# High and low parts of the up and down projections' weights, made for two units in one operation

## The reference, cut to what matters

```
h = rms_norm(x, norm2_w) * (1.0 + sc2) + sh2                     # 256 x 2048
u = causal_depthwise_conv(h @ w_up, conv_w, conv_b)              # w_up: 2048 x 11264
gate, up = u[..., :D_FF], u[..., D_FF:]                          # D_FF = 5632
x = x + g2 * ((silu(gate) * up) @ w_down)                        # w_down: 5632 x 2048
return rms_norm(x, final_norm_w)
```

## Time and profile before

| | us |
|---|---|
| three runs | 1325.77, 1335.37, 1335.42 (median 1335.37) |
| the profiled execution, its own time | 1326.2 |
| its span, first to last instruction | 1324.4 |
| up projection, PE from first to last matmul | 580.35 to 1069.9 |
| down projection, PE from first to last matmul | 1073.77 to 1312.07 |

### The profile page before, as it was taken

The page is one execution under the profiler, slowest core; times in us unless marked ns, Lnnn a source line. Parts: engine busy times, 40 slices in busy tenths (PEclk is TensorE's granted clock), DMA queues, the critical chain, the costliest instruction groups (busy, mean ns, idle before and its releaser), DMA issues.

```text
span 1324.4 us, 20876 instructions
## 1 busy us (share of the span) xinstructions
PE 1274.0 (96%) x7330; PEld 1123.7 (85%) x7330; DVE 997.0 (75%) x1277; ACT 612.8 (46%) x809; POOL 51.3 (4%) x99
## 2 busy tenths in 40 slices
PE   4899999999999999979999999999999999999996
PEld 4898999998998778868888888888888878888885
DVE  3787698998877788878887888788777765545453
ACT  3333654444546654455444444444444443434342
POOL 2000000022121000000000000000000000000000
PEclk9689999999999999989999999999999999999998
DMA  9999688888778789849777777777666675555552
GB/s 339 387 385 359 227 308 270 259 278 271 251 255 275 258 299 387 295 122 320 246 243 231 241 233 238 235 236 225 191 189 190 190 264 196 193 191 193 195 195 100
DMA packets 151716, 329.77 MB, mean 249 GB/s; under 512 B 11237, under 2 KB 11990, under 8 KB 150754
## 3 DMA queue, kind: packets, MB, share of 16 engines
q1 hardware_dynamic: 147856, 318.09, 72.3%
q0 software_dynamic: 3360, 9.98, 2.1%
q10 hardware_dynamic: 434, 0.83, 0.2%
HBM read 323.09 MB, written 4.19 MB: 247 GB/s over the span
## 4 chain that ended last, share of the span: by engine, by line
PE 85%; DVE 5%; ACT 3%; DMA 3%; issue 3%; SPq 0%; DVEq 0%; ACTq 0%
PE bank L1179 24%; PE bank L1181 13%; PE bank L1200 6%; PE bank L1201 6%; PE bank L1202 6%; PE bank L946 5%; PE bank L948 5%; PE bank L947 5%; PE bank L935 3%; PE bank L933 3%; PE bank L936 3%; DMA pc<-in_w_ada 2%; DVE acc_c L1303 2%; PE bank L980 1%; PE bank L967 1%
## 5 line engine op out<-in xcount | busy, mean ns | idle before, releaser
L618 ACT ACTIVATE whi<-wraw 128x1024 fp32r<-128x1024 f32 x408 | 432.2, 1060 | 631.9 <-PE bank L1181 234.7
L1291 DVE TENSOR_TENSOR wlo<-wraw,whi 128x1024 fp32r<-128x1024 f32 x404 | 493.8, 1223 | 258.0 <-ACT whi L618 255.9
L1179 PE MATMUL bank<-h,whi 128*128 128x512 f32 x1408 | 489.5, 392 | 2.7 <-issue 2.7
L1181 PE MATMUL bank<-h,wlo 128*128 128x256 f32 x1408 | 394.8, 280 | 0.0
L1179 PEld LDWEIGHTS bank<-h,whi 128*128 128x128 f32 x1408 | 264.0, 187 | 60.9 <-issue 2.9
L1181 PEld LDWEIGHTS bank<-h,wlo 128*128 128x128 f32 x1408 | 266.8, 189 | 0.0
L933 PE MATMUL bank<-h,whi 128*128 128x256 f32 x512 | 149.3, 292 | 3.3 <-DVE h L1316 3.3
L935 PE MATMUL bank<-h,whi 128*128 128x256 f32 x512 | 146.5, 286 | 0.0
L936 PE MATMUL bank<-h,wlo 128*128 128x256 f32 x512 | 146.5, 286 | 0.0
L1200 PE MATMUL bank<-whi,act_hi 128*128 128x512 f32 x352 | 137.0, 389 | 0.3 <-DVE evt L1580 0.3
L1202 PE MATMUL bank<-whi,act_lo 128*128 128x512 f32 x352 | 136.9, 389 | 0.0
(11 more groups left out here) (223 smaller groups left out, 1305.7 us busy)
## 6 DMA issues: line engine op xcount, KB each, us to landing
wraw<-in_w_up SPq DMA_DIRECT2D x176, 512.0 KB, 4.4
araw<-in_w_ada SPq DMA_DIRECT2D x128, 512.0 KB, 5.2
wraw<-in_w_in SPq DMA_DIRECT2D x112, 512.0 KB, 4.4
wraw<-in_w_down SPq DMA_DIRECT2D x88, 512.0 KB, 3.8
pc<-in_w_ada SPq DMA_DIRECT2D x64, 512.0 KB, 11.4
wraw<-in_w_out SPq DMA_DIRECT2D x32, 512.0 KB, 6.0
x<-in_x SPq DMA_DIRECT2D x2, 1024.0 KB, 6.8
x<-in_x POOLq DMA_DIRECT2D x1, 2048.0 KB, 11.9
```

The source lines that it names most:

```text
L618: act.activation(whi[:, slot], wraw[:, slot], ACT.Copy).then_inc(s_hi, 1)
L1179: pe.matmul(out, whi[:, slot, k, cols], h[:, kk].rearrange("p a t -> p (a t)"), start=(kk == 0), stop=False, skip_group_check=True)
L1181: last = pe.matmul(out[:, 0:SEQ], wlo[:, slot, k, cols], h[:, kk, 0, :], start=False, stop=(kk == KT - 1), skip_group_check=True)
L1291: dve.tensor_tensor(wlo[:, slot], wraw[:, slot], whi[:, slot].bitcast(F32), ALU.subtract).then_inc(s_lo, 1)
```

## The change

On ACT, `hi_pair` replaces `hi_part` from the ninth unit of the up projection to the end of the down projection: at even j one operation of 2048 elements for the slots `slot` and `slot + 1`, which waits for both loads and for PE to be through with the older unit of the second slot (`slot_free(..., j + 1)`), and adds 2 to `s_hi`. On DVE, `lo_pair` does the same for the low parts and adds 2 to `s_lo`. At odd j neither engine splits anything. SP, PE, POOL and all other work keep their code. The units of the input and output projections and the first eight of the up projection are still made singly.

```diff
--- before.py
+++ after.py
@@ -617,9 +617,17 @@
                     act.wait_ge(s_pe, ready)
                 act.activation(whi[:, slot], wraw[:, slot], ACT.Copy).then_inc(s_hi, 1)
 
+            def hi_pair(slot, count, ready):
+
+                act.wait_ge(s_w[slot], count)
+                act.wait_ge(s_w[slot + 1], count)
+                act.wait_ge(s_pe, ready)
+                act.activation(whi[:, slot:slot + 2], wraw[:, slot:slot + 2], ACT.Copy).then_inc(s_hi, 2)
+
             def hi_ahead(ph, unit0, i, j, pe0, loads):
 
-                hi_part((unit0 + j) % RING, i * loads + ((unit0 + j) // RING + 1) * 16, slot_free(ph, pe0, j))
+                if j % 2 == 0:
+                    hi_pair((unit0 + j) % RING, i * loads + ((unit0 + j) // RING + 1) * 16, slot_free(ph, pe0, j + 1))
 
 
             act.wait_ge(s_prmT, 1)
@@ -851,8 +859,8 @@
                         act.wait_ge(s_convg, 11)
                         act.activation(evt[:], bank[:, 4:8, 256:512], ACT.Copy).then_inc(s_evt, 1)
                     unit = ph.unit0 + g * ph.units + j
-                    if unit < ph.unit0 + ph.groups * ph.units:
-                        hi_part(unit % RING, (unit // RING + 1) * 16, slot_free(ph, ph.pe0 + g * ph.pe_per, j))
+                    if unit < ph.unit0 + ph.groups * ph.units and j % 2 == 0:
+                        hi_pair(unit % RING, (unit // RING + 1) * 16, slot_free(ph, ph.pe0 + g * ph.pe_per, j + 1))
                     if g == 0 and j == AHEAD + 5:
                         act.wait_ge(s_prod, 11)
                         act.activation(act_hi[:, NF - 4:, :], up[:], ACT.Copy).then_inc(s_acthi, 1)
@@ -1289,6 +1297,13 @@
                 dve.wait_ge(s_hi, unit)
                 dve.wait_ge(s_pe, ready)
                 dve.tensor_tensor(wlo[:, slot], wraw[:, slot], whi[:, slot].bitcast(F32), ALU.subtract).then_inc(s_lo, 1)
+
+            def lo_pair(unit, slot, ready):
+
+                dve.wait_ge(s_hi, unit)
+                dve.wait_ge(s_pe, ready)
+                dve.tensor_tensor(wlo[:, slot:slot + 2], wraw[:, slot:slot + 2], whi[:, slot:slot + 2].bitcast(F32),
+                                  ALU.subtract).then_inc(s_lo, 2)
 
             def first_piece(i):
                 c, r = i // KT, i % KT
@@ -1613,8 +1628,8 @@
 
                 pe0 = (i * 2 + half) * ph.pe_per + ph.pe0
                 for j in range(AHEAD, 8 + AHEAD):
-                    if j >= AHEAD + first:
-                        lo_part(i * 16 + (ph.unit0 + half * 8 + j + 1), j % RING, slot_free(ph, pe0, j))
+                    if j >= AHEAD + first and j % 2 == 0:
+                        lo_pair(i * 16 + (ph.unit0 + half * 8 + j + 2), j % RING, slot_free(ph, pe0, j + 1))
                     if finished:
                         conv_step(i if half else i - 1, 1 - half, j - AHEAD)
                     if with_ada and j % 4 == 1:
@@ -1650,8 +1665,8 @@
                     if g == 0 and j == AHEAD:
                         conv_step(last, 1, 0)
                     unit = ph_down.unit0 + g * ph_down.units + j
-                    if unit < ph_down.unit0 + ph_down.groups * ph_down.units:
-                        lo_part(unit + 1, unit % RING, slot_free(ph_down, pe0, j))
+                    if unit < ph_down.unit0 + ph_down.groups * ph_down.units and j % 2 == 0:
+                        lo_pair(unit + 2, unit % RING, slot_free(ph_down, pe0, j + 1))
                     if g == 0 and AHEAD < j < AHEAD + 7:
                         conv_step(last, 1, j - AHEAD)
                     if g == 0 and AHEAD + 9 <= j < AHEAD + 13:
```

## The result

The changed kernel takes 1343.5 us (median; 1342.4 to 1344.3 in 4 runs), the kernel before 1330.6 in the runs beside it (1325.2 to 1335.4 in 4). The ratio is 1.010, 95% interval 1.006 to 1.014: a little slower, by about 1%. Three executions of the kernel before that were disturbed (over 2400 us) are left out of every comparison. The two profiled executions differ by more, 1341.6 against 1324.4 us of span.

What follows compares the result with a forecast made beforehand. PE, busy throughout both projections, was taken as the bound. Stalls of 5.1 (rounding), 3.3 (late load), 1.7 (half clock) and 1.9 us (passage) sum to 12.0 on the 1335.4 median: 1347 us, range 1335 to 1361.

Steps and rivals of the forecast that it cites:

- Cost of the operations: The new 2048-element split operations: 1.91 us on ACT and 2.29 us on DVE.
- the chain: Slot release to PE's start on a pair: ready at S + 4.67, wanted at S + 5.55; slack falls 5.7 to 0.9 us.
- (b): ACT's rounding of the product delays the high pair of j = 10: eleven PE stalls, 5.1 us in all.
- (c): Near 610 us, unit 10 waits for unit 11's load, late when x1 is written out: 3.3 us.
- (d): Granted clock of 0.50 for 3.4 us after the idle time in (c), once: 1.7 us.
- (e): Passage to the down projection: step 0 stands behind the double low part, delaying PE once by 1.9 us.
- (a): DVE's work between low pairs, with modulation pieces: j = 6 0.40 late, j = 8 0.33, inside the slack; no stall.
- (f): Loads issued in pairs: hidden with 0.8 to 1.3 us to spare; cost taken 0.
- if PE's unit itself changes from 2.77: Sign of being wrong, in the profile after: PE's unit length differs from 2.77 us.
- Rival 3: Faster: DVE's 128 fewer operations give time back if DVE paced PE in the stretch with pieces; 1322 us, chance 0.03.
- rival 2: The chain becomes the bound in every pair, through dearer operations or late second loads; 1352 to 1370 us, chance 0.20.
- rival 1: Slack covers more: (c) falls to 1.3 without clock loss, (b) to 3; total 2 to 7 us, 1337 to 1342, chance 0.17.

Runs made afterwards that it cites:

- the order with one rhythm: PE's two 512-column matmuls, then its two of 256, per column tile in the up projection: kernel before so altered 1327.9 us, changed kernel so altered 1341.8.
- all three places mended: Changed kernel with rounding behind the next high pair, single units to 11, step 0 ahead of the last up-loop pair: 1336.9 us; with other matmul order also, 1330.7.

## Why the prediction was right, and where it was not

The forecast was 1347 us, 1335 to 1361, with a change of +12.0 us, and 0.57 for within 1%. Measured: 1343.5, and +12.9 between the medians. Point by point:

**What bounds the kernel** holds. The split took 20.0 us less of DVE, as I had said, 0.155 us for each operation saved (and DVE's busy time, which counts overlap once, fell by 13, 997.0 to 984.0), and ACT's busy time fell by 25. None of it reached PE; the time went up.

**Cost of the operations** holds to 0.01 us, and so does **the chain** of a plain pair: in the changed kernel's trace it is ready 0.9 to 1.0 us before PE needs it. The fall of the slack from 5.7 to 0.9 us is what turned three harmless delays into stalls.

**(b) The rounding** is right in place and count (the "8 waits" of the page are seven of these and the late load) and was under-sized by 1.1 us in all. At the unit length I had assumed, a stall was 1.0 us and not 0.56. The reason lies on DVE, in these lines of the changed kernel:

```profile
728.78 1.22 DVE L1595 TENSOR_TENSOR evt<-bank,evt 128x1024 f32<-128x1024 f32 x1
730.26 1.39 DVE L1600 TENSOR_SCALAR up<-evt,prm 128x256 f32<-128x256 f32 x4 [0.26 <-DVE evt L1595]
...
734.96 1.66 DVE L1605 SCALAR_TENSOR_TENSOR up<-evt,prm,up 128x255 f32<-128x255 f32 x4
736.77 1.67 DVE L1610 SCALAR_TENSOR_TENSOR up<-evt,prm,up 128x254 f32<-128x254 f32 x4
```

Where a step must wait for the end of the one before, I had added 0.11 us. The distances are 1.48 and 1.81 us where I had 1.25 and 1.69, together 0.35 more; the low pair of j = 4 stood another 0.15 late, and the product was done 0.50 us later than in my sum. In the long rhythm, where PE needs the unit 4 x 0.054 = 0.2 us later and the next unit is long in any case, a stall was 0.63 to 0.67. In the order with one rhythm all ten together were 7.7 us.

**(c) The late load** was 2.7 us, not 3.3. The load landed 0.4 us earlier, counted from PE's first matmul of the projection, and PE started 0.06 us behind the low pair and not 0.15. What I had not seen is the other side of the difference: when PE comes to unit 10 depends on how long the half clock lasts at the start of the projection, and that made the stall anything from 0.1 to 2.9 us in the experiments. As a term of a sum it needed both ends.

**(d) Half clock**: right price (1.6 us), wrong place. It came after the passage, in all five traces in which PE waited 2.3 us there, and not in the one with 1.4 us. None of the stalls near 610 (waits of 2.0 to 2.6 us) brought one, but the wait of 2.5 us near 588 with single units did. So the length of the idle time alone, by which I had placed it, does not say where it comes.

**(e) The passage**: 2.0 against 1.9. PE's wait was 2.3 us in five traces, 1.4 with pairs on DVE alone as summed, and gone in the two in which step 0 stood ahead of the last pair.

**(a) and (f), no cost**, hold for the changed kernel, but (a) was too tight. By the same distances the low pair of j = 6 started 0.8 us late near 733 us, not 0.4, which left 0.24 us between its end and PE's need where my sum leaves 0.6. In the two kernels with all three places mended, what was left cost 1.4 us (in the trace, at equal unit length) and 2.8 (between the medians): DVE's lateness and late loads, which I had counted apart.

**The term that was missing** is PE's rhythm. I had noticed that the profiled execution was 9.2 us below the median and wrote that nothing in one profile explains it. The runs showed what it is: a unit of 2.773 or 2.827 us. I had also named "if PE's unit itself changes from 2.77" as a sign of being wrong, and that sign came true, though not by the change's operations: the changed kernel's execution spent 120 of its units in the long rhythm, 6.5 us that stand in no term.

**Luck.** The stalls, which are what the sum forecast, were 12.5 us in the trace and 13.9 in the order with one rhythm, against 12.0. That also the difference of the medians came out at 12.9 is luck in part: the median of the kernel before lies between its levels, and the changed kernel is 17.8 us above the lower and 8.3 above the upper one. The base of the forecast, 1335.4, was the upper level, because two of three runs stood there; it was 4.8 us above the median of four.

**Rival 3**, faster by the freed time of DVE, did not occur; **rival 2**, a wait in every pair, neither. The lower end of **rival 1**, 2 us, does not follow from its own terms, which with (e) come to 6.2.

What stays open: why PE's unit has two lengths, and what at the start of the up projection or at a restart picks one. It was shown that no operation of the change is needed for either, that the length changed both ways at stalls of one trace, and that with two matmuls of 512 columns behind each other neither of the two lengths held and no execution reached the upper level. The matmul of 512 columns followed by one of 256 takes 346.7 ns in the short rhythm and 353.4 in the long one (2.773 and 2.827 us over eight).

## What to carry to other kernels

When producers run ahead of the bound engine through a ring, merging two of their operations saves time only on engines that are not the bound, and takes slack from the one that is: here the ring of four slots had 5.7 us of slack with single units and 0.9 with pairs. Before such a change, list what delays the producers once in a while (a copy that waits for another engine, a transfer that is late, work at a stage's end), add up those that can meet, and compare them with the new slack, not with the old. And when an unchanged kernel runs on two levels, compare unit lengths in two traces before explaining a difference of the same size.

## What the runs showed of the hardware

The unit of the up projection (eight times a matmul of 512 columns and one of 256) took either 2.773 or 2.827 us, at full granted clock, without any wait, for hundreds of us on end; the whole kernel's two levels, 1325.7 and 1335.2 us, are 9.5 us apart, and 173 units of the one and of the other length differ by 9.3. Three traces on the lower level and one on the upper show them. The down projection's unit, twelve matmuls of 512 columns, was 2.72 us in every trace, and the up projection's with another order 2.787 in both of its single-unit and its paired form. A wait of 2.5 us early in the up projection, with 3.4 us at a granted clock of 0.50 behind it, was followed by the long unit in the trace, and all ten executions of that kernel were on or above the upper level.

The first 2.9 to 6.1 us of the up projection ran at a granted clock of 0.50, differently from one trace to the next (2.9 and 6.1 in two of the unchanged kernel), and the first two units took 7.0 to 8.4 us accordingly, but for the one trace with a stall there. Near 730 us of the changed kernel's trace a VectorE operation that needs the result of the one just before it started 0.26 us after that one's end, where operations that do not wait started about 0.08 us before it.
